# Five recurrent turns inside the last tile of a first projection, with six output units' low parts made between them

## The reference, cut to what matters

```python
u = rmsnorm(x, g) @ w_in                       # 1024 x 2048
xb, gate = split(u)
xc = causal_conv(xb, width 4)
i = sigmoid(block_diag(xc, w_gx) + b_gx); r = sigmoid(block_diag(xc, w_ga) + b_ga)
a = exp(8 * r * log_sigmoid(lam))
h[t] = a[t] * h[t-1] + sqrt(1 - a[t]**2) * i[t] * xc[t]
x = x + (h * silu(gate)) @ w_out
k, v = split(rmsnorm(x, g_kv) @ w_kv)          # k is normed per head
```

## Time and profile before

| what | value |
|---|---|
| median of 3 runs | 1619.05 us (1617.78 to 1621.24) |
| profiled execution | 1617.59 us, of it span 1615.8 us, mean granted clock 0.978 |
| PE, DVE, ACT, POOL busy | 94%, 72%, 44%, 21% of the span |
| chain that ended last | PE 63%, DVE 18%, issue 7% |
| last tile of the first projection | about 325 to 400 us |
| recurrent stage | up to about 810 us |
| second projection, attention | to about 1210 us, to the end |

### The profile page before, as it was taken

The page is one execution under the profiler, slowest core; times in us unless marked ns, Lnnn a source line. Parts: engine busy times, 40 slices in busy tenths (PEclk is TensorE's granted clock), DMA queues, the critical chain, the costliest instruction groups (busy, mean ns, idle before and its releaser), DMA issues.

```text
span 1615.8 us, 31117 instructions
## 1 busy us (share of the span) xinstructions
PE 1513.2 (94%) x10752; PEld 1439.6 (89%) x10752; DVE 1159.9 (72%) x2212; ACT 706.7 (44%) x1576; POOL 336.3 (21%) x240
## 2 busy tenths in 40 slices
PE   7999999998499999998889999999996899999999
PEld 7999999998489999998879999999994688888888
DVE  7865565677499999998865846648457777777771
ACT  5322132134867667762334424334234444444440
POOL 0000000035565555554321000000122111111110
PEclk9999999999699999999899999999997999999999
DMA  6322122153223333334432212112523343333412
GB/s 239 116 81 68 64 85 67 58 174 112 86 85 106 105 97 103 109 92 158 147 104 72 76 51 81 54 62 76 164 85 104 94 116 92 108 88 102 117 47 79
DMA packets 161967, 158.45 MB, mean 98 GB/s; under 512 B 54832, under 2 KB 154928, under 8 KB 161840
## 3 DMA queue, kind: packets, MB, share of 16 engines
q1 hardware_dynamic: 149712, 147.44, 30.2%
q10 hardware_dynamic: 12128, 9.39, 1.8%
HBM read 102.68 MB, written 54.36 MB: 97 GB/s over the span
## 4 chain that ended last, share of the span: by engine, by line
PE 63%; DVE 18%; issue 7%; ACT 3%; DMA 3%; SPq 1%; POOL 1%; DVEq 0%; ACTq 0%; POOLq 0%
PE bank L651 19%; PE s_banks L651 19%; PE bank L1473 11%; DVE r_th L952 4%; PE s_banks L1410 3%; DVE r_x_hi L976 2%; PE bank L1425 2%; PE bank L1455 2%; PE bank L1213 2%; PE bank L1459 1%; PE bank L635 1%; DVE r_x L972 1%; PE s_banks L1182 1%; ACT m_p L1653 1%; DVE b_qstd L534 1%
## 5 line engine op out<-in xcount | busy, mean ns | idle before, releaser
L705 POOL TENSOR_TENSOR w_lo_a<-w_raw_a,w_hi_a 128x1024 fp32r<-128x1024 f32 x24 | 57.9, 2425 | 706.5 <-ACT w_hi_a L700 706.5
L1653 ACT ACTIVATE m_p<-s_banks,m_nm 128x192 f32<-128x192 f32 (+2 forms) x264 | 106.0, 414 | 182.9 <-DVE m_nm L1524 182.9
L1473 PE MATMUL bank<-m_y_hi,w_hi_a 128*128 128x256 f32 (+1 forms) x512 | 150.2, 293 | 0.6 <-DVE m_out L1584 0.6
L1473 PE MATMUL bank<-m_y_lo,w_hi_a 128*128 128x256 f32 (+1 forms) x512 | 145.5, 284 | 0.0
L1473 PE MATMUL bank<-m_y_hi,w_lo_a 128*128 128x256 f32 (+1 forms) x512 | 145.4, 284 | 0.0
L483 ACT ACTIVATE a_out<-a_out 128x352 f32<-128x352 f32 x48 | 24.0, 500 | 255.5 <-DVE a_out L573 255.5
L651 PE MATMUL bank<-a_hi,w_hi_a 128*128 128x352 f32 x384 | 126.1, 328 | 9.8 <-DVE w_lo_a L705 9.6
L651 PE MATMUL s_banks<-b_hi,w_hi_a 128*128 128x352 f32 x384 | 130.4, 340 | 0.0
L651 PE MATMUL bank<-a_hi,w_lo_a 128*128 128x352 f32 x384 | 124.7, 325 | 0.0
L651 PE MATMUL bank<-a_lo,w_hi_a 128*128 128x352 f32 x384 | 124.6, 324 | 0.0
L651 PE MATMUL s_banks<-b_lo,w_hi_a 128*128 128x352 f32 x384 | 124.1, 323 | 0.0
(11 more groups left out here) (204 smaller groups left out, 4909.5 us busy)
## 6 DMA issues: line engine op xcount, KB each, us to landing
w_raw_a<-weights_dram SPq DMA_DIRECT2D x32, 512.0 KB, 4.6
w_raw_b<-weights_dram SPq DMA_DIRECT2D x18, 512.0 KB, 4.2
sga_dram<-a_out SPq DMA_DIRECT2D x48, 176.0 KB, 1.9
r_xc<-xc_dram SPq DMA_DIRECT2D x32, 264.0 KB, 2.9
r_sg<-sga_dram SPq DMA_DIRECT2D x32, 264.0 KB, 2.8
r_x<-xT_dram SPq DMA_DIRECT2D x64, 132.0 KB, 2.2
x_dram<-r_x SPq DMA_DIRECT2D x64, 132.0 KB, 1.8
b_x<-x_dram SPq DMA_DIRECT2D x48, 176.0 KB, 2.3
```

The costliest lines, as they stand in the source:

```text
L705: ops.tensor_tensor(low, raw, high.bitcast(F32), ALU.subtract)\
L1473: mm = nc.tensor.matmul(out_bank(ts, blk)[:, 0:width], w[pw][:, kt * P:(kt + 1) * P], (m.y_hi, m.y_lo)[px][tp][:, kt, 0:width], start=(n = ...
L1653: nc.scalar.activation(m.p[:, q, k, v0:192], s_banks[:, 2 * q + e, bp * 192 + v0:(bp + 1) * 192], ACT.Exp, bias=m.nm[:, q, k:k + 1], accum ...
```

## The change

Five turns (0 to 4) go into the last tile on TensorE and ScalarE, behind units 2, 6, 8, 11 and 13. VectorE takes each one unit earlier, and a sixth (turn 5) behind unit 14. A seventh slot is added to the second group of shared ones. The units of the first projection take the extra slots first, so that the buffers of y, which lie over these, are free early; the low part of y's fourth group waits for the tile's end. One more unit (the first gate weights) is loaded and split in the first tile, and VectorE makes the low parts of the five other gate and key/value units behind units 5 to 9 of the last tile. GpSimd makes those of the output units 0 to 5 in pairs after its turns 2, 3 and 4, and 6 and 7 after turns 6 and 7. The decay constants move to the first tile, in six pieces behind units 10 to 15. SP's loads are moved with all this. The order of the y buffers and a gap keep the new layout apart; of the second projection's units the first is loaded one block earlier, and two are loaded later.

The diff, cut to its core:

```diff
-SLOTS_A, SLOTS_B, SLOTS_C = 8, 6, 2
+SLOTS_A, SLOTS_B, SLOTS_C = 8, 7, 2
...
-                    if isinstance(s, int) and m.first_weights and s == 1 and j < 2 * NB - 10:
+                    if isinstance(s, int) and m.first_weights and s == 1 and j <= 2 * NB - 10:
                         load_unit(eng, m.unit + 10 + j)
...
-        def decays(eng):
+        def decays(eng, part):
...
-                if m.first_weights and isinstance(s, int) and s == 1 and j + 6 < VECTOR_UNITS:
+                if m.first_weights and isinstance(s, int) and s == 1 and j + 6 <= 2 * NB:
                     low_part(eng, nc.vector, m.unit + j + 6)
+                if m.first_weights and isinstance(s, int) and s == PN and j >= 5 and U_GATE + j - 4 < VECTOR_UNITS:
+                    low_part(eng, nc.vector, U_GATE + j - 4)
...
-        VECTOR_UNITS = UNITS_IN_A
+        VECTOR_UNITS = U_KV + UNITS_KV
...
+        SLOTS_IN_A = [15, 16] + list(range(1, 15))
+        SLOTS_IN_B = [14, 0, 1, 2, 3] + list(range(6, 12)) + [4, 5, 12, 13, 15]
...
-            own = {(1, 1): 11, (1, 2): 12, (1, 3): 13}
+            own = {(1, 1): 13}
...
-        EARLY = {(PN, 9): 0, (PN, 13): 1}
-
-        def run_recurrent(eng, turn, last, after=None):
+        EARLY = {(PN, 2): 0, (PN, 6): 1, (PN, 8): 2, (PN, 11): 3, (PN, 13): 4}
...
+        def run_recurrent(eng, turn, done, last, after=None):
             def body(s, par):
                 for g in range(NG):
-                    if not (isinstance(s, int) and s == 0 and g < len(EARLY)):
+                    if not (isinstance(s, int) and NG * s + g < done):
                         turn(s, par, g)
...
-                if isinstance(t, int) and t == RN - 1:
-                    load_unit(eng, U_B1 + UNITS_GATE + blk, r.out_done, NB * t + blk + 1)
+                if isinstance(t, int) and t == RN - 1 and blk < UNITS_OUT_A - 2:
+                    load_unit(eng, U_B1 + 1 + UNITS_GATE + blk, r.out_done, NB * t + blk + 1)
...
+                    if isinstance(s, int) and (s, g) == (RN - 1, 0):
+                        load_unit(eng, U_B1)
...
-                for j in (0, 2):
-                    eng.wait_ge(a1.stored[place(a1, j)], stored_before(a1, 1, j))
+                for j in range(4):
+                    eng.wait_ge(a1.stored[place(a1, j)], stored_before(a1, 2, j))
...
-            project_sync(eng, a1, {0: start})
-            start_gates()
+            project_sync(eng, a1, {0: start, 1: start_gates, 7: second, 10: third, 12: fourth})
+            load_gate(1, 0)
             run_steps(eng, 2, RN - 2, RN + 2, body)
-            for u in range(U_B1 + UNITS_GATE + UNITS_OUT_A, U_OUT_B):
+            for u in range(U_B1 + UNITS_GATE + UNITS_OUT_A - 1, U_OUT_B):
                 load_unit(eng, u, r.kv_mm, NB * RN)
...
-                if isinstance(s, int) and (s, j) == (PN, NB):
-                    decays(eng)
-                if isinstance(s, int) and (s, j) in ((PN, 7), (PN, 12)):
-                    turn(0, 0, 0 if j == 7 else 1)
+                if isinstance(s, int) and s == 1 and j >= 10:
+                    decays(eng, j - 10)
+                if isinstance(s, int) and (s, j + 1) in EARLY:
+                    early_turn(turn, EARLY[s, j + 1])
+                if isinstance(s, int) and (s, j) == (PN, 14):
+                    early_turn(turn, len(EARLY))
...
+                if isinstance(s, int) and (s, g) == (0, NG - 1):
+                    eng.wait_ge(a1.proj_done, 2 * NB * PN)
...
-            low_units(eng, U_GATE, U_GATE + 7)
-            turn(0, 0, 0)
-            low_units(eng, U_GATE + 7, U_GATE + 11)
-            turn(0, 0, 1)
+            for n in range(len(EARLY)):
+                early_turn(turn, n)
+                if n >= 2:
+                    low_units(eng, U_OUT_A + 2 * (n - 2), U_OUT_A + 2 * (n - 1))
```

More of the change, by code:

```diff
@@ L227, in build @@
             r.th = b("r_th", [P, 2, 2, RT])
-            r.y_hi = [b(f"r_y_hi{i}", [P, NB, RT], F32R) for i in range(2)]
-            r.y_lo = [b(f"r_y_lo{i}", [P, NB, RT], F32R) for i in range(2)]
+            r.y_hi, r.y_lo = [None, None], [None, None]
+            for i in range(2):
+                r.y_hi[i] = b(f"r_y_hi{i}", [P, NB, RT], F32R)
+                r.y_lo[i] = b(f"r_y_lo{i}", [P, NB, RT], F32R)
             r.k = b("r_k", [P, RT])
@@ L502, in build, with step @@
         LW_STEPS = 5 + 2 * LW_TERMS + 4
-        def decays(eng):
[L507 to L511, removed]
+        def decays(eng, part):
+            done = (0, 5, 9, 13, 17, 21)[part]
+            def step(k, op):
                 op.then_inc(lw_step, 1)
-                eng.wait_ge(lw_step, steps[0])
+                eng.wait_ge(lw_step, done + k)
             e, z, z2, acc, tmp = (lw[:, k, :] for k in (1, 2, 3, 4, 5))
[L516 to L528, removed]
@@ new lines, in decays @@
+            if part == 0:
+                eng.wait_ge(lw_act, 2)
+                step(1, nc.vector.tensor_scalar(tmp, e, 2.0, None, ALU.add))
+                step(2, nc.vector.reciprocal(tmp, tmp))
+                step(3, nc.vector.tensor_tensor(z, e, tmp, ALU.mult))
+                step(4, nc.vector.tensor_tensor(z2, z, z, ALU.mult))
+                step(5, nc.vector.memset(acc, 1.0 / (2 * LW_TERMS + 1)))
+            elif part <= LW_TERMS // 2:
+                for i in range(2):
+                    k = LW_TERMS - 1 - 2 * (part - 1) - i
+                    step(2 * i + 1, nc.vector.tensor_tensor(acc, acc, z2, ALU.mult))
+                    step(2 * i + 2, nc.vector.tensor_scalar(acc, acc, 1.0 / (2 * k + 1), None, ALU.add))
+            else:
+                step(1, nc.vector.tensor_tensor(acc, acc, z, ALU.mult))
+                step(2, nc.vector.tensor_scalar(tmp, vec[:, LAM, :], -1.0, 0.0, ALU.mult, ALU.max))
+                step(3, nc.vector.scalar_tensor_tensor(out=tmp, in0=acc, scalar=2.0, in1=tmp, op0=ALU.mult,
+                                                       op1=ALU.add))
+                nc.vector.tensor_scalar(neg_decay[:, :], tmp, -4.0, None, ALU.mult)
+                nc.vector.tensor_scalar(decay[:, :], tmp, 4.0, None, ALU.mult).then_inc(lw_step, 1)
@@ L859, in body @@
                         load_next(pair, 0)
-                    if known(s, 0, RN - 1) and not (isinstance(s, int) and s == 0 and g < 2):
+                    if known(s, 0, RN - 1):
                         load_gate(s, g)
@@ L1157, in turn @@
                     scan_input(*one)
-            low_units(eng, U_GATE, U_GATE + 7)
-            turn(0, 0, 0)
-            low_units(eng, U_GATE + 7, U_GATE + 11)
-            turn(0, 0, 1)
+            for n in range(len(EARLY)):
+                early_turn(turn, n)
+                if n >= 2:
+                    low_units(eng, U_OUT_A + 2 * (n - 2), U_OUT_A + 2 * (n - 1))
             def after_slot(s, g):
-                if isinstance(s, int) and s < RN:
-                    for unit in recurrent_units(s, g):
-                        low_units(eng, unit, unit + 1)
-            run_recurrent(eng, turn, RN + 1, after_slot)
+                if isinstance(s, int) and s == 1 and g >= 2:
+                    low_units(eng, U_GATE + 10 + g, U_GATE + 11 + g)
+            run_recurrent(eng, turn, len(EARLY), RN + 1, after_slot)
         def recurrent_tensor(eng):
```

39 lines of the change are left out of this document (25 added, 14 removed).

## The result

The changed kernel took 1607.27 us (median of 4 runs, 1603.48 to 1610.72), the kernel before 1618.93 beside it: a ratio of 0.9926, 95% interval 0.9901 to 0.9951. A second set of 5 runs of the same code gave 1609.18 and 0.9953 [0.9936, 0.9969]. The profiled execution is the slowest of its set, 1610.72 (span 1608.9), against 1617.59 (span 1615.8): 6.87 us less from profile to profile.

A forecast was written before the change was run, and what follows sets the result against it. VectorE bounds the steady stage; no engine is full in the hole before it, where a chain of waits runs. Marker -10.0, tile 1 +1.5, loads 0 sum to -8.5 us from the median 1619.05: 1610.6; 8-in-10 range 1599 to 1617.

The forecast's parts named there:

- serial rings: Forecast case, last tile: from turn 3 on the engines' steps run one after another; gain 3.2 to 15 us; chance 0.63.
- tile 1: First tile: a low part and a decay piece before VectorE's unit 11 delay TensorE's unit 15; cost 1.5 us.
- Marker: VectorE's first residual after the last tile: forecast at 436.9 against 446.9, 10.0 us earlier, the kernel's end moving as much.
- The ring: Last tile, one serial round through VectorE, ScalarE and GpSimd: 9.65 + 1.0 + 2.4 + 1.35 + 1.6 + 0.35 = 16.3 us.
- rival 4: Last tile: slower, a loss once a ring is over 20.6 us; at 24, marker 454 and 1626 us; chance 0.06.
- The hold's rule: VectorE in the last tile: one GpSimd duration lost for each GpSimd operation that meets a VectorE operation on SBUF.
- TensorE's idle time: Sign in the last tile: idle 5 us before the gates of turns 4 and 5, about 8 before the first output matmul.
- The input of turn 7: After the tile: SP brings it at 431, before VectorE needs it at 433.8, margin 2.8 us.
- Loads: SP's moved weight loads, end of the recurrent stage: 1.5 us each, once removed, once added; net 0, bounds -2 and +3.
- The tables: ScalarE: 1.28 us load before each function change; with the skill's 1.38 us drain nothing would be gained, 1618.9 us.
- Rival 2: Last tile: TensorE is the bound and turns hide; gain 23 us, 1596 us; chance 0.13 with all gains over 15.
- The bound: Last tile: with no GpSimd operation in the rings' path, 8 us more is gained, 1602 us.

The follow-up runs named there:

- experiment 1: Changed kernel with turns 3 and 4 behind units 10 and 12 instead of 11 and 13; 1603.58 us, ratio to the kernel before 0.9914.
- experiment 8: Changed kernel with five turns in even places 2, 6, 8, 10, 12 and VectorE making the six output low parts; 1595.93 us, ratio to before 0.987.
- Experiment 6: Changed kernel, same places, with the six output units' low parts made by VectorE instead of GpSimd; 1598.76 us, ratio to before 0.9877.
- experiment 3: Changed kernel with GpSimd's low parts of output units 2 to 5 moved behind turns 5 and 6, and 6 and 7 behind turn 7; 1610.33 us.
- experiment 4: Changed kernel with the decay pieces behind units 11 to 15 of the first tile instead of 10 to 15; 1607.75 us in a single execution.
- experiment 2: Changed kernel with only turns 0 to 2 in the tile on TensorE and ScalarE, six low parts in a row on GpSimd; 1604.45 us.
- experiment 5: Changed kernel with six turns in the tile, places 2, 6, 8, 10, 12, 14, low parts still GpSimd's; 1602.39 us, ratio to before 0.9913.
- experiment 7: Changed kernel with six turns in even places, output low parts on VectorE and decay pieces one unit later in the first tile; 1593.66 us.

## Why the prediction was right

The forecast (1610.6, faster by serial rings) held; the median came 3.3 us below it, and the profiled execution lost 6.87 us where the sum had 8.5. The mechanism is the one that was forecast; two of the sum's terms were off, and one agreement is luck (tile 1, below).

- **Marker** (c, d): 438.4 with tile 1's cost, measured 440.05. The casts were to end at 393.2, 409.5 and 425.8 with that cost; the operations behind them start at 392.68, 410.17 and 427.56. Turn 3 came 0.5 early, each ring was mis-sized (16.3, measured 17.5 and 17.4), and the last leg was 12.6 and is 12.5. In the tile, then, 8.3 us were gained for a forecast of 10.0.
- **The ring, term by term**: evacuation to squared decay 9.65, measured 392.68 to 402.35, 9.67. The high copy was 1.04 for 1.0. GpSimd's low part was 2.63 for 2.4. The term that was mis-sized is the ring, and the step that failed in it is that the output product would follow the input's low part at once: the second pair of scans, 0.34 and 0.55 us alone, took 2.41 and 1.64 beside GpSimd, and the product then waited 0.79 for VectorE. That wait, the 0.23 of the low part and 0.12 of the output product (1.72 for 1.6) are most of the 1.2 us that a ring was longer. I had given the low part a place in GpSimd's line but no hold on the scans in the ring. I did price that hold for turn 3, and in rival 4.
- **The hold's rule**: in experiment 1 the three taps of unit 14 took 5.82 for 1.83 beside 4.92 us of low parts, so 4.0 us were lost; a pair of scans lost 3.2 in the ring above. The Trainium skill (SBUF — State Buffer, "Who interferes with whom") names operations with two SBUF inputs, among others; by that the trace agrees, the scans included. Operations with one input are held too: in the changed kernel the first tap of unit 10 (L613), 0.46 us alone, took 2.49 beside a pair of low parts. The evacuations of the gate units (L581), one of whose two inputs is a bank of PSUM, kept to 0.51 to 0.53 us, all 48 of them, in every kernel here.
- **TensorE's idle time**: 5 us before the gates of turns 4 and 5, 8 before the first output product; measured 5.09 and 4.22 (9.3 in two waits) and 7.6.
- **Tile 1** (e): 1.5 forecast and 1.51 in unit 15's wait. That the last tile started 1.45 later is luck: 0.85 of it was there at unit 9 of the first tile (47.26 before, 48.11 changed), ahead of the added work, and from unit 9 to the last tile the changed kernel took only 0.6 us more (283.24 for 282.64). So some 0.9 of the 1.5 came back over the tiles between, in which TensorE never waits in either kernel; why is open.
- **The input of turn 7** (f): I had it at 431 with a margin of 2.8. It came at 434.45, 3.4 us later: 1.5 of that is tile 1's cost, which the count left out, and 1.8 is the lateness of the rings, which delays the last gate's SiLU and with it this load. What VectorE needs it for hangs on the same ring and moved too: the cast of the input ended at 434.88, one-minus started at 437.27, 2.4 us of margin.
- **Loads** (f): net 0 was right within what can be seen. The five weight loads take their place behind the last k store, and the next input load is 6.03 us earlier, the marker 6.84: 0.8 us, where I had 0 between -2 and +3.
- **The tables**: the load is 1.28 us again, and the next ACTIVATE starts 0.02 after it (394.69 to 395.99). The Trainium skill (ScalarE: Activation LUTs, "What ACT_TABLE_LOAD costs") has 1.38 us more for a drain; here the measurement decides, as no such time stands between the square root's input and its start, and the leg with two loads came out at 9.67 without it.
- **Rival 2** (turns hide behind TensorE): in the changed kernel no ring was near it. In experiment 8, with order and low parts both changed, TensorE runs through the tile without a stop, but then stands idle for 11.3 us: the marker isn't TensorE's there either. **Rival 4** (slower at a ring over 20.6 us): its mechanism, holds on the scans, was real and made the rings 1.1 to 1.2 us longer, not 4.
- **The bound** "no GpSimd operation in the ring's path" was 8 us more gain, 1602. Experiment 6 took the weights' low parts off GpSimd, though not the input's and the output product: 9.4 us at the marker, 9.2 in the tile distance, 1598.76.

What stays open: why 2 us appear or vanish between residual 32 and the first attention product from one kernel to the next (-4.65 at the last residual, -8.39 at the attention). No experiment was aimed at it.

## What to carry to other kernels

When a step is moved under other work, write down for each place who waits for whom in both directions: a turn that comes behind a unit on one engine and before it on another makes a ring, and its length, not the busy time of any engine, is what each such turn costs. Low priority work given to an idle engine isn't free where that engine stands in the ring and its operations hold another engine's: here 6 units at 2.4 us on GpSimd cost 9.2 us, and on VectorE at 1.2 us, in time that it had spent waiting, nothing in the length of a ring (14.3 us in experiment 6 with them, and in experiment 3 without). That holds while VectorE has a wait to put them in: in experiment 8 it had next to none left. And look at a fixed point just behind the change and at a second one further on: experiment 3 won 5.3 us at the first and had 1.2 left at the second. Look at one ahead of the change as well: of the 1.8 us that experiment 4 seemed to bring, 0.9 were there before its edit began.

## What the runs showed that I had not expected

- Taking two of five turns out of the tile, with the low parts in one row (experiment 2), made the tile distance 2.5 us shorter than leaving them in.
- A GpSimd operation of 2.4 to 2.6 us holds even copies of 2 or 3 columns on VectorE: in experiment 5 one of 2 columns took 1.08 us, and elsewhere in the same trace 0.16.
- The time from the first attention product to the end of the span runs from 387.9 us (experiments 1, 2, 3, 5 and 8) to 393.4 (experiment 7; 390.6 before, 392.1 in the changed kernel), with the same code there and a mean granted clock of 0.983 in experiment 1 and 0.982 in experiment 7. That is larger than what several of the edits are worth: the medians of experiments 5 and 1 are 1.2 us apart, and only their markers and tile distances order them.
